# Refills by quarters in the first two steps, late pairs by quarters, and combinations between the last columns, in one hybrid layer with grouped experts

## The reference, cut to what matters

```python
def grouped_moe(x, w_router, b_router, w1, w3, w2):
    s = jax.nn.sigmoid(xt @ w_router)                 # 32 experts, 8 groups of 4
    sel = (s + b_router).reshape(t, N_GROUPS, EXPERTS_PER_GROUP)
    g_idx = jnp.argmax(lax.top_k(sel, TOP_K)[0].sum(-1), axis=-1)
    ...                                               # top 2 inside the group, gates
    def expert_block(args):
        tok, e = args
        xb = x_pad[tok]
        hb = jax.nn.silu(xb @ w1[e]) * (xb @ w3[e])   # [tokens, 512]
        return hb @ w2[e]                             # [tokens, 2048]
    ...                                               # sum over the two experts of a token

h = layer_norm(DEEPNORM_ALPHA * h + mix, ln1_g[l], ln1_b[l])
ffn = grouped_moe(h, w_router, b_router, w1[l], w3[l], w2[l])
h = layer_norm(DEEPNORM_ALPHA * h + ffn, ln2_g[l], ln2_b[l])
```

## Time and profile before

| | us |
|---|---|
| median of 3 runs | 1318.96 |
| the profiled execution, its own time | 1318.82 |
| its span | 1317.1 |
| projections, until the last matmul of L574 | 353 |
| PE busy in the span | 1245.7 (95%) |
| weights' queue q1 | 470 MB, 88.1% of 16 engines' span |

### The profile page before, as it was taken

The page is one execution under the profiler, slowest core; times in us unless marked ns, Lnnn a source line. Parts: engine busy times, 40 slices in busy tenths (PEclk is TensorE's granted clock), DMA queues, the critical chain, the costliest instruction groups (busy, mean ns, idle before and its releaser), DMA issues.

```text
span 1317.1 us, 15734 instructions
## 1 busy us (share of the span) xinstructions
PE 1245.7 (95%) x6894; PEld 719.8 (55%) x6894; DVE 436.1 (33%) x622; ACT 314.1 (24%) x529; POOL 10.8 (1%) x18
## 2 busy tenths in 40 slices
PE   5999999999999999999999999999899999999984
PEld 5989999988754444444444434434444443434431
DVE  7788895755341102111020111102020111102027
ACT  6344333533421121111221111111211111111201
POOL 2000000000000000000000000000000000000000
PEclk8999999999999999999999999999999999999997
DMA  8565554596879999999999999999999999999993
GB/s 283 189 211 181 172 191 162 179 341 248 317 313 396 379 424 429 427 427 428 428 427 428 427 427 427 427 428 428 427 427 428 427 427 428 428 427 427 428 391 134
DMA packets 68393, 472.31 MB, mean 359 GB/s; under 512 B 7666, under 2 KB 8242, under 8 KB 40930
## 3 DMA queue, kind: packets, MB, share of 16 engines
q1 hardware_dynamic: 67890, 470.47, 88.1%
q10 hardware_dynamic: 432, 0.79, 0.2%
HBM read 469.14 MB, written 2.10 MB: 358 GB/s over the span
## 4 chain that ended last, share of the span: by engine, by line
PE 74%; DMA 22%; DVE 2%; ACT 0%; SPq 0%; issue 0%; DVEq 0%
PE psum L786 29%; PE psum L547 16%; DMA ring<-in_w_dram 11%; DMA slot<-in_w_dram 11%; PE psum L574 8%; PE psum L716 7%; PE psum L825 6%; PE psum L750 2%; PE psum L751 2%; PE psum L864 1%; PE psum L773 1%; PE psum L693 1%; DMA area_a<-in_x_dram 1%; DVE area_b L1716 0%; DVE area_b L1711 0%; PE psum L513 0%
## 5 line engine op out<-in xcount | busy, mean ns | idle before, releaser
L786 PE MATMUL psum<-ring,area_c 128*64 128x512 f32 x1536 | 456.8, 602 | 22.0 <-DMA ring<-in_w_dram 11.5
L786 PEld LDWEIGHTS psum<-ring,area_c 128*64 128x64 f32 x1536 | 137.5, 138 | 231.6 <-issue 229.9
L825 PE MATMUL psum<-ring,area_d 128*64 128x512 f32 x688 | 203.2, 594 | 9.0 <-ACT area_d L1135 6.1
L547 PE MATMUL psum<-in_high,w_high 128*128 128x256 f32 x576 | 164.7, 286 | 4.1 <-DVE in_low L1240 4.1
L1611 DVE TENSOR_TENSOR area_a<-area_a,psum 128x512 f32<-128x512 f32 x60 | 41.3, 688 | 382.3 <-PE psum L751 380.7
L1115 ACT ACTIVATE area_c<-psum,gain 128x128 f32<-128x128 f32 x256 | 96.5, 461 | 296.7 <-PE psum L716 296.7
L547 PE MATMUL psum<-in_low,w_high 128*128 128x256 f32 x576 | 163.9, 285 | 0.0
L547 PE MATMUL psum<-in_high,w_low 128*128 128x256 f32 x576 | 163.9, 285 | 0.0
L1255 DVE TENSOR_TENSOR w_low<-ring,w_high 128x2048 fp32r<-128x2048 f32 x56 | 128.4, 2293 | 80.9 <-ACT w_high L962 80.9
L962 ACT ACTIVATE w_high<-ring 128x2048 fp32r<-128x2048 f32 x56 | 107.3, 1916 | 163.9 <-PE psum L547 96.3
L716 PEld LDWEIGHTS psum<-one_hot,area_b 128*128 128x128 f32 x1024 | 119.5, 195 | 13.1 <-issue 12.2
(11 more groups left out here) (186 smaller groups left out, 1008.5 us busy)
## 6 DMA issues: line engine op xcount, KB each, us to landing
ring<-in_w_dram SPq DMA_DIRECT2D x126, 2048.0 KB, 25.7
slot<-in_w_dram SPq DMA_DIRECT2D x21, 2048.0 KB, 28.7
area_g<-in_w_dram SPq DMA_DIRECT2D x21, 2048.0 KB, 24.3
ring<-in_w_in_dram SPq DMA_DIRECT2D x40, 1024.0 KB, 5.0
ring<-in_w_dram SPq DMA_DIRECT2D x26, 1024.0 KB, 8.4
ring<-in_w_out_dram SPq DMA_DIRECT2D x16, 1024.0 KB, 5.2
slot<-in_w_dram SPq DMA_DIRECT2D x6, 1024.0 KB, 6.5
area_g<-in_w_dram SPq DMA_DIRECT2D x6, 1024.0 KB, 9.2
```

The lines of the kernel that those rows point to most:

```text
L547: mm = pe.matmul(o[:, c, :], w[a][:, k, c * P:(c + 1) * P], in_part[b][:, kk, :], start=kk == 0 and a + b == 0 and c % 2 == 0, stop=kk == ...
L786: mm = pe.matmul(psum[i * CAP:(i + 1) * CAP, j // UNITS, :], gathered[:, kk, i * CAP:(i + 1) * CAP], w[i][:, k, :], start=kk == 0, stop=kk ...
L825: mm = pe.matmul(psum[i * CAP:(i + 1) * CAP, 4 + c, :], hidden_t[:, f, i * CAP:(i + 1) * CAP], w[i][:, c, :], start=f == 0, stop=f == FT - 1)
```

## The change

- `SPLIT_FILLS` goes from 20 to 32: fills 20 to 31 also go by quarters, each issued a unit after another, as the ring had it for 9 to 19.
- `load_pair` issues fills 182 to 187 by quarters, the first quarters of a pair ahead of its second ones; the second quarters have semaphores of their own (`second_rows`), and PE waits for them only at the odd m.
- In step 0 `gather` of group 3 moves from behind unit 1 to behind unit 2, with spread rows of chunk 2 right behind it. Chunk 3 moves between the second and the third block of hidden rows, into banks 0 and 1; DVE's `scaled_x1(3)` moves behind `hide(0)`. In later steps the order is as before.
- `spread_rows` multiplies by a column of the identity that is broadcast over 128 partitions, with 128 rows of `router_w`, where it had 8 of each.
- At the end the last two combinations of step 14 stand behind the first and the second pair of wide products.

```diff
-    SPLIT_FILLS = 20
+    SPLIT_FILLS = 32
+        SPREAD_BANKS = (6, 4, 6, 0)
-            refills += [((EXTRA + SLOTS + 1,), EXTRA + 1), ((EXTRA + SLOTS + 2, EXTRA + SLOTS + 3), EXTRA + 2)]
+            refills += [((EXTRA + SLOTS + 1,), EXTRA + 1)]
+            refills += [((m, m + 1), m - SLOTS) for m in range(EXTRA + SLOTS + 2, SPLIT_FILLS, 2)]
...
-                    unit_used(0, held, r)
+                    unit_used(held // STEP_UNITS, held % STEP_UNITS, r)
...
+            def load_pair(m, j, pair):
+
+                for r in range(2):
+                    for i in range(2):
+                        sp.dma_start(quarter_of(m + i, r), half_matrix(j + i, pair)[:, r * D:(r + 1) * D]).then_inc(
+                            loaded[slot_of(m + i)] if r == 0 else second_rows[(m - LATE) // 2], 16)
+
+            unit_used(PAIRS - 2, SLOTS - 2)
+            load_pair(LATE, SLOTS - 2, PAIRS - 1)
+            for j in range(0, SLOTS // 2, 2):
                 last_unit_used(j)
-                load_expert_unit(LAST + SLOTS + j, SLOTS + j, PAIRS - 2)
+                load_pair(LAST + SLOTS + j, SLOTS + j, PAIRS - 2)
...
-                    one_row = ident[0:2 * NC, r * NC + c:r * NC + c + 1].to_broadcast([2 * NC, P])
-                    mm = pe.matmul(psum[:, b + r, :], one_row, rows_1, start=True, stop=True)
+                    one_row = ident[:, r * NC + c:r * NC + c + 1].to_broadcast([P, P])
+                    mm = pe.matmul(psum[:, b + r, :], one_row, router_w[:, 0:CW], start=True, stop=True)
...
+                elif LATE <= m < LATE + 6:
+                    pe.wait_ge(second_rows[(m - LATE) // 2], 16 * 2)
...
                         gather(it, s, 2)
+                    if j == (2 if first else 1):
                         pe.wait_ge(slot_gates_kept, it + 1)
                         gather(it, s, 3)
+                        if first:
+                            spread_rows(2)
...
-                    if first and 3 <= j < 5:
-                        spread_rows(j - 1)
...
                     hidden_rows(f, arrived(STEP_UNITS * it + 2 * UNITS + f))
+                    if first and f == 1:
+                        pe.wait_ge(gt_drained, 1)
+                        spread_rows(NC - 1)
...
-                for c in range(NC):
-                    combine_apart(a, c)
+                combine_apart(a, 0)
+                combine_apart(a, 1)
...
+                    if f < 2:
+                        combine_apart(a, 2 + f)
```

More of the change, by code:

```diff
@@ L227, in hybrid_layer @@
         loaded = [sem(f"expert_half_loaded{i}") for i in range(SLOTS)]
+        second_rows = [sem(f"late_second_quarters_loaded{i}") for i in range(3)]
         extra_loaded = sem("extra_half_loaded")
@@ L270, in slot_of @@
             return m if m < EXTRA else (m - 1) % SLOTS
+        LATE = STEP_UNITS * PAIRS - SLOTS - 2
         def arrivals(m):
@@ L410, in _ @@
                 load_expert_unit(m, m % STEP_UNITS, m // STEP_UNITS)
-            for j in range(SLOTS):
+            for j in range(SLOTS - 2):
                 unit_used(PAIRS - 2, j)
                 load_expert_unit(LAST + j, j, PAIRS - 1)
-            for j in range(SLOTS // 2):
+            def load_pair(m, j, pair):
[6 more added lines that the diff above has]
+            for j in range(0, SLOTS // 2, 2):
                 last_unit_used(j)
-                load_expert_unit(LAST + SLOTS + j, SLOTS + j, PAIRS - 2)
+                load_pair(LAST + SLOTS + j, SLOTS + j, PAIRS - 2)
             def load_columns(m, at, i, f, first, end, signal):
@@ L682, in spread_rows @@
             def spread_rows(c):
-                b = 6 - 2 * (c % 2)
+                b = SPREAD_BANKS[c]
                 if c == 0:
@@ L688, in spread_rows @@
                     pe.wait_ge(logits_fixed, 1)
-                else:
-                    pe.wait_ge(x1_ready, c - 1)
+                elif c == 2:
+                    pe.wait_ge(x1_ready, 1)
                 for r in range(2):
-                    one_row = ident[0:2 * NC, r * NC + c:r * NC + c + 1].to_broadcast([2 * NC, P])
-                    mm = pe.matmul(psum[:, b + r, :], one_row, rows_1, start=True, stop=True)
+                    one_row = ident[:, r * NC + c:r * NC + c + 1].to_broadcast([P, P])
+                    mm = pe.matmul(psum[:, b + r, :], one_row, router_w[:, 0:CW], start=True, stop=True)
                 mm.then_inc(rows_spread, 1)
@@ L840, in step @@
                 if first:
-                    pe.wait_ge(x1_ready, NC)
+                    pe.wait_ge(x1_ready, NC - 1)
                 else:
@@ L845, in step @@
                     hidden_rows(f, arrived(STEP_UNITS * it + 2 * UNITS + f))
+                    if first and f == 1:
+                        pe.wait_ge(gt_drained, 1)
+                        spread_rows(NC - 1)
+                if first:
+                    pe.wait_ge(x1_ready, NC)
             def step_again(i2, s):
@@ L895, in last_two_steps @@
                         last_rows(f, c, [wide[i][:, f, c, :] for i in range(2)], s_wide)
+                    if f < 2:
+                        combine_apart(a, 2 + f)
                 for f in range(FT):
+                    if f == 0:
+                        pe.wait_ge(y_drained, NC * b)
                     if f == FT - 1:
@@ L1664, in _ @@
                 if it == 0:
-                    for c in range(NC):
+                    for c in range(NC - 1):
                         scaled_x1(c)
-                    dve.wait_ge(x1_ready, NC)
                 if 0 < it < PAIRS - 1:
@@ L1670, in _ @@
                 hide(it, it == PAIRS - 1)
+                if it == 0:
+                    scaled_x1(NC - 1)
+                    dve.wait_ge(x1_ready, NC)
             keep_y_low(PAIRS - 2, 0)
```

## The result

The changed kernel takes 1311.18 us (median of 4 runs, 1308.51 to 1311.78) against 1319.01 of before beside it (4 runs). The ratio is 0.9935, with a 95% interval of 0.9918 to 0.9952. The forecast was 1309.9, the range 1307.3 to 1313.3. The profiled execution took 1308.51 us for a span of 1306.8.

A forecast was written before the change was run, and what follows sets the result against it. The stream of weights was taken to set the pace from 461 us on. The terms, -3.8 + 1.6 - 1.7 - 3.2 - 1.9 = -9.0, from 1318.82 + 0.1 give 1309.9 us; eight in ten between 1307.3 and 1313.3.

The forecast's parts named there:

- B: Step 0, gather 3, spread rows and chunk 3 moved: the queue runs dry and the stream comes later, +1.6 us.
- C: Fills 20 to 31 by quarters: holes between 418 and 460 us close, less a price for smaller pieces, -1.7 us.
- A: Full-array spread rows in step 0 keep PE's clock up, so gathers, unit 0 and refills come sooner, -3.8 us.
- rival 1: The clock falls all the same near the ranking; gain at most -1.0, total 1312.7 us; chance 0.17.
- rival 4: Nothing gained before 461 us: spread rows fail, the gather move eats the quarters' gain; 1317 to 1321 us; chance 0.04.
- The 0.7 us charged for smaller pieces: Fills 20 to 31: quarters at 422 against 427 GB/s, 1.2% of 59 us, cost 0.7 us.
- rival 3: Quarters of fills 20 to 31 run slowly, at 294 GB/s, +26.7 us, total 1337; chance 0.04.
- D: Fills 182 to 187 by quarters: one block of 3.5 us stays behind the last weights instead of 7.09, -3.2 us.
- The 0.35 us charged for pieces of 1.05 MB: Late pairs by quarters: the last weights land later by 1.2% of 29 us, 0.35 us.
- E: Two combinations of step 14 between the last columns: waits of the third and fourth for `y_low` go, -1.9 us.
- rival 2: The last columns bind: late column pieces give back about 3 us, total 1312.9; chance 0.09.
- The signs that I had listed: Profile checks: gathers 3.7 us, unit 0 at 365.5, dips near 388 and 420, last columns near 1287.

The follow-up runs named there:

- e10: Changed kernel with two filler matmuls around the ranking and the spread rows back on 8 partitions; 1312.57 us, 0.9956 of before.
- e3: Changed kernel with the spread rows back on 8 partitions, no fillers; 1312.70 us, 0.9960 of before.
- e11: Changed kernel unchanged, profiled a third time, one run; 1311.24 us.
- e12: Changed kernel unchanged, profiled a fourth time, one run; 1310.92 us.
- e9: Kernel before with the full-array spread rows as its only change; 1316.30 us, 0.9981 of before.
- e5: Kernel of e2 with fills 20 to 31 whole again; 1311.82 us, 0.9948 of before.
- e4: Changed kernel with gather 3 behind gather 2 and spread rows of chunk 2 behind unit 3 again, chunk 3 left moved; 1310.20 us, 0.9942 of before.
- e8: Kernel of e2 with gather 3 and spread rows of chunk 2 moved back, chunk 3 left moved; 1306.80 us, 0.9913 of before.
- e2: Changed kernel plus two filler matmuls, results unused, in PE's gaps around the ranking; 1309.22 us, 0.9929 of before.
- e6: Kernel of e2 with fills 182 to 187 whole again; 1312.06 us, 0.9953 of before.
- e7: Kernel of e2 with all four combinations of step 14 ahead of the last columns again; 1311.26 us, 0.9940 of before.
- e1: Changed kernel unchanged, measured again with five runs; 1309.29 us, 0.9934 of before.

## Why the prediction was right, point by point

The time lay 1.3 us above the forecast and inside its range, and the mechanisms named are the ones that the runs show. Two things were luck: the errors of B and C cancelled, and the median depends on which group of executions was drawn. By its steps:

**A, the spread rows: right in about half the executions.** The step said that 128 rows keep the clock up, -3.8. e10 shows that the rows in use, and not idle time, made the old fall. In profiles where the clock is kept A is worth 3.6 against the one profile of before; against e10 and e3, where the fall lasted 6.8 us and not 10.2, it is 2.8 and 2.1 (in e10 the fillers at half clock are a part of that). The gathers begin 6.1 us behind the first spread row for 7.0, as said. The step put that down to ACT's normalising; in after that ends at 360.1 us, they begin at 360.3 behind DVE's one-hot, so the two bind nearly together. But rival 1 isn't the other case that I took it for. It happens *as well*, in the second group (e11, e12) and in e9: the clock falls a little later, in the ranking, for 3.4 us, where before it is low for 10.2, as this window of before has it:

```profile
358.20:368.40 10.20, 9.42 (x35) 7.29 (x35) 7.53 (x30) 4.90 (x7) 0.00 (x0) 0.50 0.90 376
```

I had priced it at 2.8 us (all gathers at half clock), and it costs 1.6, since a good part of the gathers then still runs at the full clock. This step is the mis-sized one: -3.6 in one group, -2.0 in the other, where one number stood. The step looked at what stood before the old fall and not at the next place where PE is nearly idle, 3 us behind it, though the earlier trace rows held a fall behind idle time, at 764.4. How busy PE was doesn't settle it alone: in before it kept its clock behind 1252.5 us with 1.71 of 3.5 us, and in e11 it lost it with 1.88 of 3.4.

**B and C: each one undersized, the sum right by luck.** Together they are -0.8 us of L, the mean over nine profiles with both, for -0.1. The whole of B costs 2.3 on the old refills (e5 against before and e9, 899.7 for 897.4), where +1.6 stood. e4 and e8 take back only its part at the gathers and leave chunk 3 in the hidden rows; that part is worth 1.5 (e2 against e8). The remaining 0.8 would then be what chunk 3 costs where it now stands, by the later refills of 18 to 21; no run moves chunk 3 alone, so this isn't shown. C is -3.4 (e2 against e5), where -1.7 stood. With these sizes e8 against before should be -3.4 + 0.8 = -2.6, and it is -2.6. The second half of rival 4, that B eats C, is thus true for two thirds of C. What failed in C is the reading: I took the idle part of three windows by their DMA share, 2.4 us. By their rate, 294, 251 and 400 of 427 GB/s, the same windows hold 1.9 + 2.5 + 0.8 = 5.1 us. The change left most of the first of these (303 GB/s over 418 to 422 us in after) and closed the other two but for 0.3, so about 3.0 by this reading; the chip shows 3.4. The 0.7 us charged for smaller pieces wasn't to be seen: over 424 to 442 us they run at 424 GB/s. By that rival 3 falls. With it falls the figure of the Trainium skill (DMA: Bandwidth & Descriptors, Bandwidth) for one transfer of 1 MB, 341 GB/s, as a guide to pieces queued behind each other.

**D, the late pairs: right.** -3.2 forecast, -3.4 by the profile, 2.8 us by the medians of e6 and e2. The 0.35 us charged for pieces of 1.05 MB weren't there.

**E, the combinations: mechanism right, a little small.** -1.9 forecast, -1.5 by the profile, 2.0 us by the medians of e7 and e2. The third and the fourth combination of step 14 waited for `y_low` in before:

```profile
1276.95 0.50 PE L764 MATMUL psum<-y_high,one_hot_t 128*128 128x512 f32 x1 [1.05 <-DVE y_low L1604]
1278.75 0.50 PE L764 MATMUL psum<-y_high,one_hot_t 128*128 128x512 f32 x1 [0.60 <-DVE y_low L1604]
```

In after one such wait is left, and it is not theirs. It is that of the last combination of step 15, at 1287.5 us, and before has it too (0.30 at 1297.8):

```profile
PE psum L784 <- DVE y_low L1634: 0.3, 1, 0.3
```

So the four combinations take 2.06 + 1.13 + 1.13 = 4.3 us where they took 6.1, -1.8. What the step left out is that the products between them, now in three stretches, take 1.87 + 1.87 + 6.16 = 9.9 us where 9.59 stood, +0.3.

Rival 2 has nothing for it: no wait of PE for `ring` stands at L890.

**The sum.** A -3.6 or -2.0, B and C -0.8, D -3.4, E -1.5 give -9.3 or -7.7: from 1318.9, 1309.6 or 1311.2. The second group came at 1310.9 to 1311.8, as it should, though A's two sizes are taken against the one profile of before. The first came at 1308.5 to 1309.7; its start 1.5 us earlier, which isn't the change's doing, takes it from 1309.6 to 1308.1, L in after was 0.6 over its mean, and the fall at 1261.4 in e1 gave 1.7 back. That accounts for the profiled ones alone. So the median depends on how many executions of each group are drawn, 1311.18 in the first measurement and 1309.29 in the second. Differences under 2 us between these kernels are therefore taken from the four lengths, not from medians.

The signs that I had listed came as said: the gathers at 3.8 us, PE's stand ahead of unit 2 (1.52 for 1.7), the hole near 388 and the dip near 420, the hidden rows' end 3.65 us behind the last wait, PE's waits in steps 6 to 13, the first whole fill issued at 483.5 us. Unit 0 came at 364.2 for 365.5, by the earlier start, and the last columns ended at 1286.1 for about 1287.

## What to carry to other kernels

Size a hole in a stream of DMAs by its GB/s against the full rate, and not by the busy share of the engines: the share hid half of the idle time here. When an edit removes one fall of TensorE's clock, look at once at the next place where the engine stands, for the fall can move there in some executions; two products that compute nothing in such a gap are cheap. Where one program's times fall into two groups, price the parts by lengths between fixed points of the profile, and take more profiles until both groups have been seen. When two moves share one step of the forecast, as gather 3 and chunk 3 do in B, undo each alone as well.

## What the runs showed of the hardware that was not expected

- The same program kept TensorE's clock at 2.4 GHz through the ranking in two profiles and fell to 1.2 GHz for 3.4 us in two others (gathers of 3.84 and 5.47 us). The same holds for the start of the program: a mean clock of 0.84 and 0.68 over 20.4 to 31 us. The Trainium skill (TensorE: Matmul & The Clock Gate, Part 1, What's actually happening) says that the slow start differs from run to run; the two windows agree. That one program differs so in the midst of a kernel too is what after and e11 show.
- An engine that was busy all the time, with products on 8 rows of the array, lost its clock for 6.8 us (e10). With 128 rows in the same place the clock stayed up to the ranking in all eleven profiles.
- Quarters of 1.05 MB, queued behind each other, ran at 424 GB/s, as fast as pieces of 2.1 MB but for 1%.
- Single falls of the clock behind waits for weights, as at 1261.4 us in e1, come in some executions and cost up to 1.7 us where PE is on the path.
